# Values in two passes over all PSUM banks, stores on ScalarE, and expert outputs added onto the residual rows by a scatter

## What is computed

```python
h = rmsnorm(x, norm_mix)
qa, ka, va, qb, kb, vb = split(h @ w_in)
ya = swa_gqa_sinks(rope(qa), rope(ka), va, sinks) @ w_o_a
yb = chunk_relbias_attention(qb, kb, vb, rel_bias) @ w_o_b
gates = sigmoid(h @ w_branch_gate + b)
x = x + (gates[0] * ya + gates[1] * yb) @ w_out
h2 = rmsnorm(x, norm_ffn)
# 4 groups of 8 experts: top group, then the top 2 experts in it
x = x + sum over k of weight[k] * (silu(h2 @ w_eg[e_k]) * (h2 @ w_eu[e_k])) @ w_ed[e_k]
out = rmsnorm(x, norm_final)
```

## Time and profile before

| | |
|---|---|
| three runs | 2796.7, 2798.78, 2799.37 us; median 2798.78 |
| profiled execution | 2798.48 us, span 2796.7 us |
| mean granted TensorE clock | 0.921 |
| project | 0 to about 889 us |
| attend_b, attend_a | to about 1350 us |
| merge | to about 1804 us |
| route | to about 1845 us |
| experts | to about 2697 us |
| combine | to 2796.7 us |
| busy: TensorE, DVE, ScalarE, POOL | 2352.3, 1339.7, 1049.8, 704.7 us |

### The profile page before, as it was taken

One profiled execution on the slowest core, in us unless ns is written; L12 is line 12 of the kernel. 1 busy time (PEld: TensorE's weight loads), 2 busy tenths in 40 slices (PEclk: granted clock), 3 DMA queues, 4 the chain that ended last, 5 costly groups with the idle time before them and its releaser, 6 DMA issues. The chain is left out here.

```text
span 2796.7 us, 37025 instructions
## 1 busy us (share of the span) xinstructions
PE 2352.3 (84%) x12254; PEld 1997.5 (71%) x12255; DVE 1339.7 (48%) x1962; ACT 1049.8 (38%) x1705; POOL 704.7 (25%) x693
## 2 busy tenths in 40 slices
PE   3899996899996888838199999749999999999940
PEld 2788875688885777738199999638888888888830
DVE  7201122200000777727433333367866767777958
ACT  4211111111111777726222222135645646666722
POOL 4255555530000000000132222013322322333442
PEclk6899998999998999959599999869999999999975
DMA  4255566681113555287654444358866868888958
GB/s 144 75 143 165 189 203 176 177 338 68 67 68 114 145 146 145 70 175 167 213 149 144 147 144 137 112 193 295 327 231 227 316 230 315 307 329 320 387 223 327
DMA packets 238591, 548.57 MB, mean 196 GB/s; under 512 B 56032, under 2 KB 90272, under 8 KB 232496
## 3 DMA queue, kind: packets, MB, share of 16 engines
q1 hardware_dynamic: 191120, 409.12, 44.6%
q0 software_dynamic: 27056, 89.67, 9.8%
q10 hardware_dynamic: 20336, 48.77, 4.7%
HBM read 413.46 MB, written 134.02 MB: 196 GB/s over the span
## 5 line engine op out<-in xcount | busy, mean ns | idle before, releaser
L394 DVE TENSOR_TENSOR pj_w_lo<-pj_w_raw,pj_w_hi 128x1024 fp32r<-128x1024 f32 x46 | 66.0, 1440 | 663.6 <-ACT pj_w_hi L333 663.5
L333 ACT ACTIVATE pj_w_hi<-pj_w_raw 128x1024 fp32r<-128x1024 f32 x46 | 48.6, 1059 | 643.0 <-PE pj_bank L436 524.9
L436 PE MATMUL pj_bank<-pj_hT_hi,pj_w_hi 128*128 128x512 f32 x960 | 257.6, 390 | 3.5 <-DVE pj_w_lo L394 3.5
L436 PE MATMUL pj_bank<-pj_hT_lo,pj_w_hi 128*128 128x512 f32 x960 | 257.4, 390 | 0.0
L436 PE MATMUL pj_bank<-pj_hT_hi,pj_w_lo 128*128 128x512 f32 x960 | 257.0, 390 | 0.0
L1768 POOL TENSOR_TENSOR ex_wd_lo<-weights_raw_d,ex_wd_hi 128x1024 fp32r<-128x1024 f32 x64 | 194.4, 3058 | 131.7 <-ACT ex_wd_hi L1793 131.7
L436 PEld LDWEIGHTS pj_bank<-pj_hT_hi,pj_w_hi 128*128 128x128 f32 x960 | 180.6, 188 | 41.3 <-DVE pj_w_lo L394 3.9
L436 PEld LDWEIGHTS pj_bank<-pj_hT_lo,pj_w_hi 128*128 128x128 f32 x960 | 180.8, 188 | 37.7
L436 PEld LDWEIGHTS pj_bank<-pj_hT_hi,pj_w_lo 128*128 128x128 f32 x960 | 180.7, 188 | 37.6
L1415 PE MATMUL mg_y_ps<-mg_aT_hi,mg_w_hi 128*128 128x256 f32 x512 | 149.1, 291 | 56.7 <-DVE mg_aT_lo L1327 49.0
L1858 DVE TENSOR_TENSOR ex_wd_lo<-weights_raw_d,ex_wd_hi 128x1024 fp32r<-128x1024 f32 x64 | 169.1, 2681 | 9.8 <-ACT ex_wd_hi L1793 9.8
(11 more groups left out here) (245 smaller groups left out, 5590.4 us busy)
## 6 DMA issues: line engine op xcount, KB each, us to landing
weights_raw_g<-in_w_exp_gate_dram SPq DMA_DIRECT2D x128, 512.0 KB
weights_raw_u<-in_w_exp_up_dram SPq DMA_DIRECT2D x128, 512.0 KB
weights_raw_d<-in_w_exp_down_dram SPq DMA_DIRECT2D x128, 512.0 KB
scratch_ys<-ex_y ACTq DMA_DIRECT2D x47, 512.0 KB, 4.1
pj_w_raw<-in_w_feat_dram SPq DMA_DIRECT2D x46, 512.0 KB, 6.0
scratch_gates<-pj_f_hi SPq DMA_DIRECT2D x32, 512.0 KB, 3.4
scratch_ys<-pj_g_row POOLq DMA_DIRECT2D x32, 512.0 KB, 16.3
mg_g_in<-scratch_gates SPq DMA_DIRECT2D x128, 128.0 KB, 3.0
```

Of the source, the lines that this page charges most:

```text
L333: act.activation(w_hi[n % 2][:], w_raw[n % 2][:], ACT.Copy).then_inc(whi_done, 1)
L394: dve.tensor_tensor(w_lo[n % 2][:], w_raw[n % 2][:], w_hi[n % 2][:], ALU.subtract).then_inc(wlo_done, 1)
L436: last = pe.matmul(eight[4 * p + b][:], w[p][:, k * P:(k + 1) * P], h[:, k, b * NB:(b + 1) * NB], start=(k == 0 and n == 0), stop=(k == KD ...
```

## The change

**project.** V_STEPS goes from 4 to 2 and a TOKENS step now fills all eight banks, with 8 token tiles; the four value weight tiles are loaded twice instead of four times, and a piece holds 48 matmuls instead of 24. The matmuls of a piece go bank by bank, six in a row into one. All stores of the stage move from SP to ScalarE. A value tile is stored in one DMA of 512 KB with its high and low parts side by side (runs of 128 floats); the four buffers f_hi0, f_hi1, f_lo0, f_lo1 take turns. Writing the zeros is dropped.

**route.** tile_hot carries three numbers for each row instead of one: token number plus one, and the high and low part of its weight; POOL makes the third. The matmuls are 192 columns wide instead of 64. The results are routes.token, routes.target (the row of x2 that a row of y is added to; empty rows go to 128 spare rows behind x2) and routes.row_weight.

**experts.** y_out multiplies by the row's weight, and POOL adds y onto the rows of x2 by an indirect DMA with an addition; the store to ys goes. The wait for y_stored is the same.

**finish** replaces combine: no gathers, no adds; loads on SP with eight buffers, squares a tile ahead on ScalarE, stores on POOL with four output buffers.

```diff
 QK_TILES = 8
-V_STEPS = 4
+V_STEPS = 2
+V_BANKS = 8
...
-            for n, (s, c) in enumerate(PIECES):
-                if n + 2 < len(PIECES):
-
-                    sp.wait_ge(wlo_done, n + 1)
-                    sp.dma_start(w_raw[n % 2][:], w_feat[weight_tile(*PIECES[n + 2])]).then_inc(w_ready[n % 2], 16)
-                if n == last_piece(s):
-                    for half in range(2):
-                        store(s, half)
-            for half in range(2):
-                sp.wait_ge(hi_stored[half], stores_from(STEPS, False))
-                sp.wait_ge(lo_stored[half], stores_from(STEPS, True))
+            for n in range(2, len(PIECES)):
+
+                sp.wait_ge(wlo_done, n - 1)
+                sp.dma_start(w_raw[n % 2][:], w_feat[weight_tile(*PIECES[n])]).then_inc(w_ready[n % 2], 16)
...
-            pool.wait_ge(zeros_set, 1)
-            with pool.Fori(0, blank.shape[0] // P) as t:
-                pool.dma_start(blank[ds(t * P, P), :], g_row[:]).then_inc(blanked, 16)
-            pool.wait_ge(blanked, blank.shape[0] // P * 16)
...
+            def token_buffer(b):
+                return (f_hi[0], f_hi[1], f_lo[0], f_lo[1])[b % 4], (*hi_stored, *lo_stored)[b % 4]
+
+            def evacuate_tokens(s):
+                for b in range(V_BANKS + 1):
+                    if b < V_BANKS:
+                        buffer, stored = token_buffer(b)
+                        if b < V_BANKS - 1:
+                            act.wait_ge(v_done, (s - A_TILES - QK_TILES) * (V_BANKS - 1) + b + 1)
+                        else:
+                            act.wait_ge(mm_done, last_piece(s) + 1)
+
+                        act.wait_ge(stored, stores_from(s, b % 4 >= 2) + b // 4 * 16)
+                        act.activation(buffer[:].rearrange("p (h a d) -> p h a d", a=2, d=DH)[:, :, 0, :],
+                                       eight[b][:].rearrange("p (h d) -> p h d", d=DH), ACT.Copy).then_inc(f_hi_done, 1)
+                    if b > 0:
+                        buffer, stored = token_buffer(b - 1)
+                        act.wait_ge(f_lo_done, evacuations(s, (SPLIT, TOKENS)) - V_BANKS + b)
+                        hold(act, held)
+                        act.dma_start(v_b[:, :, (s - A_TILES - QK_TILES) * V_BANKS + b - 1, :, :].rearrange("h p a d -> p h (a d)"),
+                                      buffer[:].bitcast(F32).rearrange("p (h c) -> p h c", h=8)).then_inc(stored, 16)
+
             split_weights(0)
...
                 if n == last_piece(s):
-                    evacuate(s)
+                    if KINDS[s] == TOKENS:
+                        evacuate_tokens(s)
+                    else:
+                        evacuate(s)
+                        store(s)
+            for half in range(2):
...
-            def tokens(p, c, tile):
-
-                for kk in range(2):
-                    k = 2 * c + kk
-                    for n, (h, w) in enumerate(((hT_hi, w_hi), (hT_hi, w_lo), (hT_lo, w_hi))):
-                        for b in range(4):
-                            last = pe.matmul(eight[4 * p + b][:], h[:, k, ds((tile + b) * P, P)],
+            def tokens(s, c):
+
+                v = s - A_TILES - QK_TILES
+                for b in range(V_BANKS):
+                    if c == 0:
+
+                        pe.wait_ge(f_lo_done, evacuations(s - 1, (SPLIT, TOKENS)) + (b + 1 - V_BANKS if v else 4 * (b // 4) - 4))
+                    for kk in range(2):
+                        k = 2 * c + kk
+                        for n, (h, w) in enumerate(((hT_hi, w_hi), (hT_hi, w_lo), (hT_lo, w_hi))):
+                            last = pe.matmul(eight[b][:], h[:, k, ds((v * V_BANKS + b) * P, P)],
                                              w[c % 2][:, kk * NB:(kk + 1) * NB],
                                              start=(k == 0 and n == 0), stop=(k == KD - 1 and n == 2))
+                    if c == V_CHUNKS - 1 and b < V_BANKS - 1:
+                        last.then_inc(v_done, 1)
...
+            pool.wait_ge(weight_split, 1)
+            for k in range(2):
+                pool.wait_ge(tile_is_done, k + 1)
+                pool.tensor_tensor(tile_hot[k][:, :, 2, :], tile_is[k][:],
+                                   weight_lo[k][:].bitcast(F32).unsqueeze(2).broadcast_to([P, NT, MAX_TILES]),
+                                   ALU.mult).then_inc(low_hot_done, 1)
...
-            for k in range(2):
-                then(dve.tensor_scalar(routes.slot[k][:], slot_f[:, k, :], float(FRONT * P), None, ALU.add))
-
...
+                dve.wait_ge(tile_is_done, k + 1)
+                dve.tensor_tensor(tile_hot[k][:, :, 0, :], tile_is[k][:], over(ids[:], MAX_TILES),
+                                  ALU.mult).then_inc(tile_hot_done, 1)
+                dve.tensor_tensor(tile_hot[k][:, :, 1, :], tile_is[k][:], over(weight_hi[k][:].bitcast(F32), MAX_TILES),
                                   ALU.mult).then_inc(tile_hot_done, 1)
             then(dve.memset(routes.token[:, MAX_TILES:], 0))
+            then(dve.tensor_scalar(spare_row[:], ids[:, 0:1], float(SEQ), None, ALU.add))
+            then(dve.tensor_scalar(routes.target[:, :FRONT], place_row[:, :FRONT], 0.0, spare_row[:], ALU.mult, ALU.add))
+            then(dve.tensor_scalar(routes.target[:, :FRONT], routes.target[:, :FRONT], -1.0, None, ALU.add))
             dve.wait_ge(token_done, 1)
-            then(dve.tensor_copy(routes.token[:, :MAX_TILES], token_ps[:, :MAX_TILES]))
...
+            then(dve.tensor_scalar(routes.token[:, :MAX_TILES], token_ps[:, 0, :], -1.0, 0.0, ALU.add, ALU.max))
+            then(dve.tensor_scalar(before[:], token_ps[:, 0, :], -1.0, None, ALU.add))
+            then(dve.tensor_scalar(empty[:], token_ps[:, 0, :], 0.0, None, ALU.is_equal))
+            then(dve.scalar_tensor_tensor(routes.target[:, FRONT:], empty[:], spare_row[:], before[:], ALU.mult, ALU.add))
+            then(dve.tensor_copy(low_part[:], token_ps[:, 2, :]))
+            then(dve.tensor_tensor(routes.row_weight[:, FRONT:], token_ps[:, 1, :], low_part[:], ALU.add))
...
+            def add_rows(n):
+
+                pool.wait_ge(y_done, n + 1)
+                pool.tensor_copy(targets[:], routes.target[:, ds(n, 1)]).then_inc(targets_ready, 1)
+                pool.wait_ge(targets_ready, n + 1)
+                hold(pool, held)
+                pool.indirect_dma_start(out=x2, out_offset=bass.IndirectOffsetOnAxis(ap=targets[:, 0:1], axis=0),
+                                        in_=y[:], in_offset=None, compute_op=ALU.add).then_inc(y_stored, 16)
+
             def step(n):
 
+                add_rows(n)
                 pool.wait_ge(x_turned, n + 2)
...
-                store(n)
...
-                dve.tensor_copy(y[:, :NB], y_ps[0][:])
-                dve.tensor_copy(y[:, NB:], y_ps[1][:]).then_inc(y_done, 1)
+                dve.tensor_scalar(y[:, :NB], y_ps[0][:], routes.row_weight[:, ds(n + 1, 1)], None, ALU.mult)
+                dve.tensor_scalar(y[:, NB:], y_ps[1][:], routes.row_weight[:, ds(n + 1, 1)], None,
+                                  ALU.mult).then_inc(y_done, 1)
...
+            for t in range(NT):
+                pool.wait_ge(normed, t + 1)
+                pool.dma_start(out[t * P:(t + 1) * P, :], done[t % 4][:]).then_inc(stored[t % 4], 16)
+            for p in range(4):
+                pool.wait_ge(stored[p], 16 * (NT // 4))
...
+            def square(t):
+                act.wait_ge(x_ready[t % BUFS], 16 * (t // BUFS + 1))
+                if t >= 4:
+
+                    act.wait_ge(rstd_done, (t - 4) * RSTD_STEPS + RSTD_STEPS)
+                act.activation(junk[t % 2][:], x_in[t % BUFS][:], ACT.Square, accum_out=stat[t % 4][:, 0:1]).then_inc(ssq_done, 1)
+
+            square(0)
             for t in range(NT):
-                p = t % 2
-                act.wait_ge(summed, 2 * t + 2)
-                act.activation(junk[p][:], x_in[t % BUFS][:], ACT.Square, accum_out=stat[p][:, 0:1]).then_inc(ssq_done, 1)
-                root(act, stat[p], t, mean_done, root_done)
+                if t + 1 < NT:
+                    square(t + 1)
+                root(act, stat[t % 4], t, mean_done, root_done)
...
+                    mean_square(dve, stat[(t + 1) % 4], t + 1, ssq_done, mean_done)
+                inverse_rms(dve, stat[t % 4], t, root_done, rstd_done)
+                if t >= 4:
+
+                    dve.wait_ge(stored[t % 4], 16 * (t // 4))
```

183 lines of the change are left out of this document (85 added, 98 removed).

## The result

| | before | after |
|---|---|---|
| median of four runs each | 2797.78 us | 2728.70 us |
| lowest and highest | 2796.70, 2799.37 | 2726.52, 2731.55 |
| profiled execution, its span | 2798.48, 2796.7 | 2731.55, 2729.7 |

The ratio is 0.9753 with a 95% interval of [0.9736, 0.977]. The forecast of 2724 was 4.7 us too low, inside its range of 2706 to 2752. The profiled execution of the changed kernel is the slowest of its four, 2.9 above their median, so a few us of what follows are spread between runs.

A forecast was written before the change was run, and what follows sets the result against it. Bounds: value-weight stalls, DVE and DMA in the last stage, nearly full TensorE, DVE and DMA in the expert loop. From 2798.5 us, −35 (value), −48 (last stage), +6 (routing), +2 (loop end), +0.5 (stores) gave 2724; range 2706 to 2752.

The forecast's parts named there:

- signs of being wrong: DVE waiting for the scatter ahead of y, one-tile steps of 19 us up, ScalarE buffer waits, last-stage tiles over 3 us.
- Forecast 108.5 us: Value projection after the change: 89.7 matmuls, 9.0 between passes, 1 at the start, 8.8 before the gates; was 142.8.
- the four stalls: Value projection before: TensorE waited 45.3 us in four stalls for low weights, loads queued behind V stores on SP.
- I price this at zero: Value projection: ScalarE issuing all stores ahead of the next weight split costs nothing, as it idles most of the stage.
- The rival in which evacuations overlap the passes: Value projection: evacuations overlap the pass, so waits of 3.7 and 6.5 us go; 2713 us; chance 5%.
- 51.5 forecast: Last stage: 51.5 us instead of 99.5, gain 48 (42 to 53), without gathers and adds.
- +6 forecast: Routing: 2.4 for two more DVE products, 2.5 for POOL beside DVE, 1.3 for small operations; 3 to 9.
- 0 forecast: Expert loop: accumulating scatter priced like the plain store, hidden by 18 us of matmuls; cost 0.
- The ceiling: Expert loop rival: accumulate also reads its destination, 1.3 us more in each of 17 full-DMA steps; 2746 us; chance 15%.
- The late scatter: Expert loop rival: landing beyond 14.8 us delays 17 one-tile steps; at 20 us landing, 2812 us; chance 5%.
- +2: End of expert loop: last two rows' copy, gap and scatter replace a plain issue; 2 us more.
- ScalarE's last stores: Value projection: 0.5 us added for the last stores that ScalarE issues.

## Why the prediction was right, and which steps were not

The size of the sum is in part luck: three terms came out 13.5 us dearer than forecast and three 6 us cheaper, and they cancel in part. Two of the signs of being wrong showed in the trace, ScalarE's waits for stored buffers in the value part (3.19 and 2.94 us) and DVE's waits with the scatter's name; neither cost more than was priced.

**Value part: size right, reason half wrong.** Forecast 108.5 us, of which 2.3 lie behind the first gate matmul; measured 103.6, and 1.7 are given back behind that point. The gain of 35 was 38 to 39.
- The step "SP now has nothing in its queue but weight loads, so the mechanism of the four stalls is gone" is half the reason. The earlier trace rows showed a queue of stores, and I took that for the cause. With four passes, taking the stores out of it removes 24.0 of the 45.3 us; 21.3 come back in ScalarE's queue. With two passes the same queue, longer (16.5 us), costs 3.3 us. The prediction had the second half of the sentence too (loads two pieces ahead, 48 matmuls a piece), and that half carries the gain with the stores on either engine.
- Matmuls six in a row in one bank: priced at 0.2335 each from the expert loop, measured 0.227. 2.6 us too much. The expert loop's pace is its own, not that of the same bank.
- Evacuations: 3.7 and 3 (for stores) between the passes were forecast at 6.7, with 2.3 for the clock. Measured 6.8 of waits for all value matmuls; the 3.2 us wait took no clock away, but with the later ones about 4 us of slower matmuls remain. The wait ahead of the gates was 5.7 for a forecast 6.5.
- "I price this at zero" of the stores on ScalarE: with two passes this held (attention starts within 1.1 us with the stores on either queue). With four passes it does not hold: the next split waited 9.57 us behind the stores.
- The rival in which evacuations overlap the passes was rightly given little: ScalarE's order spoke against it. Reordered, it gave 16.4 us, more than the 11 it was priced at.

**Last stage: right.** 51.5 forecast, 50.0 measured, first large operation 9.7 us in instead of 9. The middle ran at 404 to 419 GB/s as the earlier trace rows said. It runs against the DMA engines, with tiles of 2.1 us at first and at the end and about 2.5 in the middle, where buffers wait for their stores. By the figure of 358 GB/s in the Trainium skill (DMA: Bandwidth & Descriptors, Specifications) it would have been 53; the trace doesn't agree. That row divides the 716 GB/s of a stack between two cores, and here one core ran.

**Routing: low by 3.** +6 forecast (3 to 9), +8.9 measured. DVE beside POOL lost 3.4 us where I took 2.5. The other 2 us come with the first gather's issue: where it takes 1.06 us, the routing is 6.8 longer. It takes 2.59 in this kernel, with the stores on SP, with the scatter twice and with the wait on ScalarE, and 1.05 or 1.06 in the other four with the new routing, though the kernel with the wait on ScalarE differs from its base (1.06) only at the end of the loop. I can't say what it hangs on; it stays open.

**Expert loop: 0 forecast, 1.5 measured, within what runs of one kernel differ.** The loop from first to last x took 827.6 us after and 826.1 before, and 826.5 to 827.9 in the others that scatter once. Two rivals were priced on it. The ceiling's premise is true: 1.6 us more of the DMA engines' time per scatter, against the 1.3 I had worked out. Over 750 us the share stands at 0.80 before, and the earlier trace rows is one dense window of 18 us. In the changed kernel it costs nothing that can be read: TensorE is busy for 18.00 of 18.00 us even where the share is 1.05 (2420 to 2438 us). The late scatter was judged by the steps with new weights alone, where 10.5 us lie between issue and next y, as worked out, and with room up to 14.8. The steps that were left out are those without new weights: there the product is ready, and y can follow, 9.4 to 10.2 us after the issue, and the scatter lands after 9.4. So it cost nothing, but it used up the room of these steps. Room behind y was left all the same: with the scatter doubled, y was 1.1 to 3.0 us later in them and TensorE lost nothing by it. What the doubled scatter met is the other rival, the DMA ceiling: the doubled scatter lost 26 us from 2386 us to the last y, with ScalarE waiting for weights. In the changed kernel neither came.

**End of the loop: the term that was mis-sized.** +2 was for a copy, a gap and an issue. Those are there (from the multiply at 2664.75 to the scatter's issue 2.6 us, where the plain store went out 1.5 after). What I did not price was the landing, because I carried it over from the plain store at zero, and what comes with the end of the block behind it: 12.35 us from issue to the next stage instead of 4.0. Of these the scatter alone takes 6.35 (the kernel with the stage inside the block), and 6.0 come with the end of the block. Together with 1.5 us of slower matmuls ahead of the last y (they start 0.43 us apart from 2657.9 to 2661.5), the end costs +11 instead of +2. Against the profiled execution the sum misses by 7.5: +9 from this term, +3 from the routing and +1.5 from the loop, less 4 from the value part, 1.5 from the last stage and 0.5 for ScalarE's last stores.

**What is open: the idle time behind POOL's last transfer.** The end of a block, or of the program, comes late in most kernels where the last DMA before it was issued by POOL:

| kernel | last DMA before the end of the block | us without data before the next one, or the end |
|---|---|---|
| before, end of experts | plain store, ScalarE | 1.8 |
| before, with a gather added | gather, POOL | 5.9 |
| after, end of experts | accumulating scatter, POOL | 6.7 |
| after, without accumulation | plain scatter, POOL | 9.7 |
| after, scatter twice | accumulating scatter, POOL | 3.7 |
| early evacuation, wait on ScalarE | accumulating scatter, POOL | 6.0 |
| stage inside the block, end of program | plain store, POOL | 8.0 |
| after, end of program | plain store, POOL | 2.9 |

It isn't the accumulation, nor that POOL itself waits (the wait on ScalarE: 11.6 against 12.3 us), nor that the last transfer is indirect. The last row speaks against a simple rule: the same kind of store from POOL ended the program after 2.9. One difference fits and has not been tested: in that last block POOL issued plain stores only, in the six above it had issued indirect transfers as well. Nor is it a fixed time behind the data, as 3.7 and 9.7 us show. All that is shown is that the wait went away, at both ends, in the kernel with no block's end after the scatter and with the last stores on SP.

## What to carry to other kernels

When a queue of stores stands ahead of a load, ask first how long the work is that the load runs ahead of. Here moving the stores to another engine took away half of the stall and gave the other half to that engine's queue, and with work twice as long per load (and half as many loads) nearly all of it went on either engine. When the profile names a transfer as what ended a wait, look how long the other thing that the same instruction needs had been ready, before calling it a cost. When a store becomes another kind of transfer, price its landing in every kind of step and once at the end of the loop, where nothing covers it, and price its load on the DMA engines where the weights come fastest. And put what frees a bank ahead of what prepares the next weights: here that was a new order on two engines, for 16 us.

## What the runs showed of the hardware that I had not expected

- An accumulating scatter of 128 rows of 4 KB takes 1.6 us to issue on POOL against 1.0 for a plain one, 1.6 us more of all DMA engines' time at the same packets and bytes, and lands 9.4 us after issue in the five steps of the loop that show it and 6.35 with nothing beside it. Two of them overlap: both have landed after 11.3 us in the step shown, and after 8.9 to 14.1 over the kernel.
- Eight value stores hold the queue that issues them whichever it is: 10.9 us on SP and 8.9 on ScalarE at 256 KB each, 16.5 on SP at 512 KB each. The instruction behind them on that engine waits as long.
- POOL slows DVE on products: 2.92 instead of 1.21 us for 128x1024 and 3.99 instead of 2.28 for 128x2048, while POOL takes 3.3 for each of its own; what POOL would take alone, no run shows.
- Six matmuls in a row into one bank with alternating weights start 0.227 us apart, as in alternation.
- One core moved 404 to 420 GB/s between HBM and SBUF in stretches of 10 us of the last stage, with loads and stores mixed.
- Before the end of a block or of the program whose last DMA came from POOL, 5.9 to 9.7 us pass with no data moving in five kernels, 3.7 with the scatter twice, and 2.9 at the changed kernel's end; the cause is open.
- The first gather of the expert loop takes POOL 2.59 us to issue in four kernels and 1.05 or 1.06 in four with the same routing or nearly so; the cause is open.
